# Sharing the operand's low halves between VectorE and GpSimd at two norms of a two-layer hybrid backbone

## What is computed

```python
def rms_norm(x, w):
    xf = x.astype(jnp.float32)
    y = xf * lax.rsqrt(jnp.mean(xf * xf, axis=-1, keepdims=True) + EPS)
    return (y * w.astype(jnp.float32)).astype(x.dtype)
...
        h = h + g1 * y.astype(h.dtype)
        u = rms_norm(h, norm_ffn_w[layer]) * (1.0 + sc2) + sh2
        h = h + g2 * conv_ffn(u, ffn_w_up[layer], ffn_conv_w[layer], ffn_conv_b[layer], ffn_w_down[layer])
```

## Time and profile before

| | us |
|---|---|
| timed executions, median of 3 | 1855.6 (1855.03 to 1863.26) |
| the profiled execution | 1852.07 |
| its span, first to last instruction | 1850.3 |

### The profile page before, as it was taken

One profiled execution on the slowest core, in us unless ns is written; L12 is line 12 of the kernel. 1 busy time (PEld: TensorE's weight loads), 2 busy tenths in 40 slices (PEclk: granted clock), 3 DMA queues, 4 the chain that ended last, 5 costly groups with the idle time before them and its releaser, 6 DMA issues.

```text
span 1850.3 us, 26061 instructions
## 1 busy us (share of the span) xinstructions
PE 1733.1 (94%) x9562; PEld 1439.2 (78%) x9562; DVE 864.2 (47%) x1351; ACT 739.8 (40%) x1165; POOL 542.7 (29%) x251
## 2 busy tenths in 40 slices
PE   4899999998979999999999979999999799999997
PEld 1677888886768888888888867878567588888876
DVE  6778876666675544444324241000773522222343
ACT  3472434774232322233333343211883333334442
POOL 1123123462212223232322213222002244444442
PEclk9899999998989999999999979999999899999998
DMA  8313223343323443334221212212321132323221
GB/s 323 133 68 131 91 78 108 122 142 132 114 69 114 137 137 125 120 119 137 69 69 58 69 34 69 69 57 68 120 75 55 48 103 91 102 91 103 92 91 46
DMA packets 66872, 184.04 MB, mean 99 GB/s; under 512 B 5952, under 2 KB 26816, under 8 KB 65744
## 3 DMA queue, kind: packets, MB, share of 16 engines
q1 hardware_dynamic: 45072, 164.69, 26.4%
q10 hardware_dynamic: 21696, 17.88, 3.2%
HBM read 180.40 MB, written 2.15 MB: 99 GB/s over the span
## 4 chain that ended last, share of the span: by engine, by line
PE 77%; DVE 6%; ACT 3%; issue 1%; POOL 0%; ACTq 0%; DMA 0%; DVEq 0%; PEldq 0%; POOLq 0%
PE ps L1812 34%; PE ps L2193 13%; PE ps L1811 9%; PE ps L1825 4%; PE ps L1882 3%; PE ps L2190 3%; PE ps L2279 2%; PE ps L2292 2%; PE ps L2267 2%; PE ps L1789 1%; DVE later_norm_nt L1191 1%; PE ps L1888 1%; DVE u L1206 1%; PE ps L1895 1%; PE ps L1796 1%
## 5 line engine op out<-in xcount | busy, mean ns | idle before, releaser
L566 POOL TENSOR_TENSOR wsp<-raw,wsp 128x1024 fp32r<-128x1024 f32 x201 | 492.7, 2451 | 1227.7 <-ACT wsp L631 1227.3
L1812 PE MATMUL ps<-u,wsp 128*128 128x512 f32 x2712 | 807.4, 396 | 12.8 <-DVE u L1203 8.5
L1812 PEld LDWEIGHTS ps<-u,wsp 128*128 128x128 f32 x2712 | 513.0, 190 | 131.8 <-DVE u L1203 9.4
L631 ACT ACTIVATE wsp<-raw 128x1024 fp32r<-128x1024 f32 x201 | 213.2, 1061 | 536.9 <-PE ps L1812 433.2
L1811 PE MATMUL ps<-u,wsp 128*128 128x256 f32 x1464 | 412.9, 282 | 9.6 <-DVE u L1206 8.9
L2193 PE MATMUL ps<-hsp,wsp 128*128 128x512 f32 x1056 | 307.9, 394 | 2.2 <-DVE hsp L1624 2.2
L1811 PEld LDWEIGHTS ps<-u,wsp 128*128 128x128 f32 x1464 | 278.1, 190 | 12.8 <-DVE u L1206 7.3
L2193 PEld LDWEIGHTS ps<-hsp,wsp 128*128 128x128 f32 x1056 | 197.6, 188 | 50.5 <-issue 3.4
L1633 DVE SCALAR_TENSOR_TENSOR conv<-apad,vec,conv 128x770 f32<-128x770 f32 (+1 forms) x44 | 48.0, 1090 | 272.8 <-ACT conv L1006 272.7
L1624 DVE TENSOR_TENSOR hsp<-hid,hsp 128x768 fp32r<-128x768 f32 (+1 forms) x88 | 83.1, 944 | 192.1 <-ACT hsp L1028 190.7
L2190 PE MATMUL ps<-hsp,wsp 128*128 128x256 f32 x528 | 146.0, 280 | 1.1 <-DVE hsp L1624 1.0
(11 more groups left out here) (240 smaller groups left out, 1813.5 us busy)
## 6 DMA issues: line engine op xcount, KB each, us to landing
raw<-in_weights SPq DMA_DIRECT2D x281, 512.0 KB, 3.6
nab<-in_nabias ACTq DMA_DIRECT2D x32, 256.0 KB, 2.8
start_w<-in_start SPq DMA_DIRECT2D x8, 512.0 KB, 15.4
start_w<-in_start SPq DMA_DIRECT2D x4, 1024.0 KB, 18.5
h<-in_x SPq DMA_DIRECT2D x4, 768.0 KB, 10.4
mD<-rows_scratch ACTq DMA_DIRECT2D x12, 256.0 KB, 4.1
mqs<-rows_scratch ACTq DMA_DIRECT2D x12, 256.0 KB, 5.0
h<-in_x ACTq DMA_DIRECT2D x2, 1536.0 KB, 7.3
```

The source lines that it names most:

```text
L566: pool.tensor_tensor(wsp[:, s % 2, 1, :], raw[:, raw_index(s) % 4, :], wsp[:, s % 2, 0, :].bitcast(F32), ALU.subtract).then_inc(*own.one(l ...
L631: act.activation(wsp[:, s % 2, 0, :], raw[:, raw_s % 4, :], ACT.Copy).then_inc(*own.one(hi_ready))
L1812: mm = pe.matmul(lat, w, x[:, k, xp, toks], start=first, stop=last)
```

## The change

At norms 1 and 3 the odd parts (1, 3, 5, 7) get another way. ScalarE adds the shift in place, in the buffer `q.nt[:, 1]`, and then copies the buffer into the high half. GpSimd subtracts the high half from the buffer, into the low half, and counts this on a semaphore of its own, `u_lo_pool`. VectorE makes the low halves of the even parts only, and before it scales part 3, 5 or 7 it waits for GpSimd's low half of part 1, 3 or 5. TensorE waits for part k on the semaphore of the engine that makes it (`low_at`). GpSimd's walk through the weight blocks is cut behind block `S_UP0 + 1` and behind block `S_UP1 + 1`, and the odd parts of norms 1 and 3 are put in there. Norms 0, 2 and 4 are as before.

```diff
+                self.shared = n in (1, 3)
+                self.lo_ready = Part(u_lo, KT * n - 4 * (n // 2))
+                self.lo_pool = Part(u_lo_pool, 4 * (n // 2))
+            def low_at(self, k):
+                if not self.shared:
+                    return self.lo_ready.at(k + 1)
+                return (self.lo_pool if k % 2 else self.lo_ready).at(k // 2 + 1)
...
-            blocks(own.loop, {lo_ready: 4}, S_MIX - S_OUT0 - 2, lambda n, i: low(S_OUT0 + 2 + n, i))
-            blocks(own.loop, {lo_ready: 4}, S_END - S_MIX, lambda n, i: low(S_MIX + n, i))
+            def low_parts(q, toks):
+
+                for k in range(1, KT, 2):
+                    pool.wait_ge(*q.hi_ready.at(k + 1))
+                    pool.wait_ge(*own.last())
+                    pool.tensor_tensor(u[:, k, 1, toks], q.nt[:, 1, toks], u[:, k, 0, toks].bitcast(F32), ALU.subtract)\
+                        .then_inc(*own.one(u_lo_pool))
+
+            blocks(own.loop, {lo_ready: 4}, N_OUT, lambda n, i: low(S_OUT0 + 2 + n, i))
+            low_parts(norm[1], slice(0, N_TOK))
+            blocks(own.loop, {lo_ready: 4}, S_MIX - S_UP0 - 2, lambda n, i: low(S_UP0 + 2 + n, i))
+            blocks(own.loop, {lo_ready: 4}, S_UP1 + 2 - S_MIX, lambda n, i: low(S_MIX + n, i))
+            low_parts(norm[3], LAT)
+            blocks(own.loop, {lo_ready: 4}, S_END - S_UP1 - 2, lambda n, i: low(S_UP1 + 2 + n, i))
...
+                    if q.shared and k % 2:
+                        for t, r in ((CTX, 1), (LAT, 0)):
+                            if r == 0 or toks != LAT:
+                                act.activation(q.nt[:, 1, t], q.nt[:, 1, t], ACT.Identity, bias=B(k, r))\
+                                   .then_inc(*own.one(act_own))
+                        act.wait_ge(*own.last())
+                        act.activation(u[:, k, 0, toks], q.nt[:, 1, toks], ACT.Copy).then_inc(*own.one(q.hi_ready.whole))
+                        continue
...
                 for k in range(KT + 1):
                     if k < KT:
+                        if q.shared and k % 2 and k >= 3:
+                            dve.wait_ge(*q.low_at(k - 2))
                         dve.wait_ge(*own.last())
...
-                    if k >= 1:
+                    if k >= 1 and not (q.shared and k % 2 == 0):
                         e = k - 1
...
-                        pe.wait_ge(*ready.at(k + 1))
+                        pe.wait_ge(*ready.low_at(k))
```

More of the change, by code:

```diff
@@ L326, in build @@
         DIRECT = (4, KT - 1, 4, KT - 1, 4)
-        acc_added, sq_ready_n, sq_summed, t_ready, u_hi, u_lo = map(sem, (
-            "acc_added", "norm_sq_ready", "norm_sq_summed", "t_ready", "u_hi", "u_lo"))
+        acc_added, sq_ready_n, sq_summed, t_ready, u_hi, u_lo, u_lo_pool = map(sem, (
+            "acc_added", "norm_sq_ready", "norm_sq_summed", "t_ready", "u_hi", "u_lo", "u_lo_pool"))
         class Norm:
@@ L341, in __init__ @@
                 self.hi_ready = Part(u_hi, KT * n)
-                self.lo_ready = Part(u_lo, KT * n)
+                self.shared = n in (1, 3)
[5 more added lines that the diff above has]
+                return (self.lo_pool if k % 2 else self.lo_ready).at(k // 2 + 1)
         norm = [Norm(n, direct) for n, direct in enumerate(DIRECT)]
@@ L2176, in up @@
                     features(s_up + b, i, ps[:, b % 2, :], cx_bank(b) if layer == 0 else None, u,
-                             n.lo_ready if b == 0 else None)
+                             n if b == 0 else None)
                 for b in range(N_UP):
@@ L2242, in _ @@
                 features(S_QK + n, 0, ps[:, n % 2, :], cx_bank(n) if n >= KT else None, u,
-                         norm[2].lo_ready if n == 0 else None)
+                         norm[2] if n == 0 else None)
             for cg in range(2):
```

## The result

The changed kernel takes 1866.19 us, median of 22 executions, against 1858.62 for the kernel before in 22 executions beside it. The ratio is 1.0041, 95% interval 1.0029 to 1.0052: 7.6 us slower, between 5.4 and 9.7, and within the 0.5% that I had called no change. The forecast was +6.4 us. Of the 4.2 us by which 1862.0 misses, 3.0 are the base, whose median moved from 1855.6 to 1858.62 with more executions.

A forecast was written before the change was run, and what follows sets the result against it. TensorE, busy 94% of the span, was taken to bound the kernel, idling for operands at norms 1 and 3. Part 7 delays (1.96, 2.0) plus clock losses (1.0, 1.4) made 6.4 us on 1855.6: 1862.0, range 1856 to 1868.

The forecast's parts named there:

- What bounds: Whole kernel: TensorE is busy 94% of the span, so only stretches where it idles can give or cost time.
- The ring: Norms 1 and 3: two parts through VectorE, ScalarE and GpSimd take 5.20 against 4.84 us, and 3.59 against 3.28.
- The handover from GpSimd to VectorE: End of each ring turn: VectorE's next odd scaling starts 0.10 us after GpSimd's subtraction, an estimate.
- the line between the two sizes: Norm 1: GpSimd's subtraction of 768 columns takes 1.84 us, read between rows for 512 (1270 ns) and 1024 (2401).
- Part 7: Last part at each norm: TensorE starts it later, by 1.96 us at norm 1 and 2.0 us at norm 3.
- The collision with the modulation: Norm 1's end: GpSimd's last subtraction and VectorE's modulation exclude each other, so it ends 0.63 us later than alone.
- The clock: TensorE at its low level for 2.8 us from part 7: +1.0 us at norm 1, +1.4 at norm 3.
- The sum: Part 7's delays and the clock's losses at norms 1 and 3 together: 6.4 us slower.
- Rival (a): Norms 1 and 3: TensorE's clock stays low through the parts and into the next blocks; 1866.4 us, chance 0.19.
- Rival (b): Norms 1 and 3: the delay mostly hides as TensorE has work to catch up; about +1.5, 1857.1 us, chance 0.10.
- Rival (c): Norms 1 and 3: VectorE's relief counts, were buffers no limit; 7.7 us less, 1847.9 us, chance 0.03.
- The Trainium skill's factor of two: GpSimd about twice as slow with two inputs: subtractions of 2.3 and 1.5 us, and a sum of 9.2 us.

The follow-up runs named there:

- norm1_only: Changed kernel with only norm 1 shared with GpSimd, norm 3 as before; ratio to the kernel before 1.001 (0.9989 to 1.0032).
- norm3_only: Changed kernel with only norm 3 shared with GpSimd, norm 1 as before; ratio to the kernel before 1.004 (1.0015 to 1.0065).
- no_collision: Changed kernel, with VectorE waiting for GpSimd's last low half before the modulation behind norms 1 and 3; ratio to the kernel before 1.0019.
- double_sub: Changed kernel, with GpSimd making each of its low halves twice, the second time over the first; ratio to the kernel before 1.0124.
- three_buffers: Changed kernel with a third buffer for the scaled parts, used by parts 3 and 7; ratio to the kernel before 0.9972.
- three_tail: Changed kernel with the third buffer, and part 7's low half back on VectorE the old way; ratio to the kernel before 0.995.

## Why the prediction was right

- *What bounds*: TensorE waits for the operand at both norms and nowhere else does the change reach it. Borne out by norm1_only and norm3_only, each of which moved its own stretch alone.
- *The ring*: predicted 5.20 and 3.59 us a turn, measured 5.10 and 3.55. The handover from GpSimd to VectorE, which no row showed and I put at 0.10, took 0.04 (521.79 + 1.82 to 523.65). GpSimd's 768 columns took 1.82, predicted 1.84 by the line between the two sizes; 512 took 1.27.
- *Part 7*: predicted +1.96 and +2.0, measured +1.56 and +1.91 in the first pair of profiles. At norm 1 that pair is not typical. The changed ring gives part 7 at 22.15 to 22.18 us in all four profiles, but unshared it came at 20.62, 20.61, 19.79 and 19.77: by TensorE's low level in the first two, as the prediction had read, and right behind its low half in the others, which were at the full level. The mean is +1.96.
- *The collision with the modulation*: predicted 0.63, measured 0.52 and removed by no_collision. I had the modulation begin 0.6 us ahead of GpSimd; it began 0.55 ahead.
- *The clock*: predicted +1.0 and +1.4, from a low stretch of 2.8 us behind part 7 at both norms. Beyond part 7 the stretches leave 3.5 - 1.96 = 1.6 and 2.8 - 1.9 = 0.9. At norm 1 no profile of the changed ring had the 2.8 us: the clock was low behind part 7 for about 6 us in three profiles and not at all in one. At norm 3 it was low for 2.2 to 2.6 us in three and not at all in one. So the sum is near, the shares are not, and one norm varies by 2.7 us between executions of one kernel. Here I was right in size by a mean over what is a draw, and that is luck.
- *The sum*: 6.4 predicted, 6.3 in the profiles' stretches, 7.6 (5.4 to 9.7) in the timed runs.
- *Rival (a)*, the clock low for long: it happened in part (6 us behind part 7 at norm 1 in three of four profiles with that ring) but never to the 5.3 us of loss it needed. The measured 1866.19 lies closer to its 1866.4 than to my 1862.0, but only because the base is 3.0 us higher; its +10.8 us is outside the measured 5.4 to 9.7. *Rival (b)*, hidden: no; double_sub shows that nothing of GpSimd's time is. *Rival (c)*, VectorE's relief: not with two buffers, as the diff has it. three_buffers made it come true in part: of the 7.7 us that I had worked out, the stretches show 2.2, the timed runs 5.2 (0.9 to 9.7). three_tail's two stretches gained 7.1.
- *The Trainium skill's factor of two* for GpSimd gave 9.2 us: measured 1.82 us against VectorE's 1.15 for the same columns, 1.6 times, and 1.27 against 0.75, 1.7 times. The rows priced it better. The advice of the Trainium skill, "GPSIMD Engine Reference", section "Engine selection", to keep such work on VectorE held in the runs with two buffers (1.0041) and not with three (0.9972).

What stays open: the timed difference of 7.6 us is 1.3 above the stretches, within its interval, and I did not trace it further. A wider reading of the six profiles of the two kernels, from norm 1's first scaling to the last weight copy without the 39 blocks whose rate varies, gives less: 982.1 us before (980.3 to 984.9) and 986.7 changed (982.7 to 989.0), so +4.6, where the two stretches of the same six give +5.7. What decides the clock's course at a norm is open too.

## What to carry to other kernels

Work taken off the busiest engine shortens a loop only if the buffers let that engine run ahead. Count the turn of each buffer through all engines that touch it and compare it with what the busy engine took for the same items before: 5.1 against 4.84 lost, and one more buffer, 3 KB a partition, won. The last item of such a loop has no cover, so leave it on the shortest way: that alone had the last low half ready 1.95 and 1.05 us earlier here.

## What the runs showed of the hardware

- TensorE has two rates in the same instructions at the same granted clock: a block of 24 products of 256 and 24 of 512 columns took 8.32 us in some executions and 8.48 in others, for either kernel, while the latent-only blocks of layer 1 took 5.44 in all. It is 6.2 us of a single span in 39 such blocks alone, and a pair of profiles alone would have been read as the change's. What sets the rate was not looked into.
- GpSimd's subtraction and a VectorE instruction with two SBUF inputs wait for each other: 2.34 us for 1.82 in the changed kernel, 2.69 in three_buffers, 1.82 again once VectorE was held back; VectorE's L1144 took 3.43 us for 1.23. VectorE's scaling, with one operand in PSUM, took 1.14 us beside GpSimd in three_buffers as always.
- Behind a norm TensorE's clock stays at the low level for anything between nothing and 6 us of unbroken work, in executions of one kernel whose engines otherwise keep the same times to 0.02 us from the first scaling on. Behind norm 1's part 7 it was none, 0.8 and 3.9 us in the kernel before, none and twice about 6 us in the changed one. What decides it was not settled.
